# Moving the SBUF addresses of a two-block transformer kernel so that all rounded matmuls have the same distance between weights and moving columns

## What is computed

```python
# first stack, for l in range(2)
proj = rms_norm(x, attn_norm_g[l]) @ w_in[l]          # 1024 -> 8932 columns
... indexed attention (a), rwkv recurrence (b), pooling (c), retention (d)
gates = sigmoid(pg.reshape(b, s, 4, 1024) + gate_b[l])
merged = sum(gates[:, :, i] * (o_i @ w_branch[l, i]))
x = x + merged @ w_out[l]
x = x + square(relu(h2 @ mlp_up[l])) @ mlp_down[l]     # 1024 -> 4096 -> 1024

# second stack, for layer in range(2)
mod = silu(c) @ mod_w[layer] + mod_b[layer]
h = rmsnorm(x, norm_mix[layer]) * (1.0 + sc1) + sh1
y = hybrid_mixer(h, ...) if layer % 2 == 0 else mla_mixer(h, ...)
x = x + g1 * y
h = rmsnorm(x, norm_ffn[layer]) * (1.0 + sc2) + sh2
x = x + g2 * peer_ffn(h, w_q, sub_keys, u, v)

# peer_ffn: each token picks 8 x 16 of 16384 experts
act = gelu(einsum('td,ted->te', h, u[expert]))
out = einsum('te,ted->td', gates * act, v[expert])
```

## Time and profile before

| | |
|---|---|
| runs of the kernel before | 3461.89, 3463.27, 3465.05 us |
| span of the profiled execution, and its own time | 3463.0 us (nothing is shown outside the span) |
| PE busy | 3382.3 us, 98% of the span |
| PEld (weight loads, beside PE) | 3057.9 us, 88% |
| DVE, ACT, POOL busy | 71%, 47%, 10% |
| PE on the chain that ended last | 88% |
| mean granted TensorE clock | 0.989 |

### The profile page before, as it was taken

One profiled execution on the slowest core, in us unless ns is written; L12 is line 12 of the kernel. 1 busy time (PEld: TensorE's weight loads), 2 busy tenths in 40 slices (PEclk: granted clock), 3 DMA queues, 4 the chain that ended last, 5 costly groups with the idle time before them and its releaser, 6 DMA issues.

```text
span 3463.0 us, 69595 instructions
## 1 busy us (share of the span) xinstructions
PE 3382.3 (98%) x24630; PEld 3057.9 (88%) x24630; DVE 2458.7 (71%) x5105; ACT 1632.7 (47%) x3275; POOL 362.4 (10%) x480
## 2 busy tenths in 40 slices
PE   8999999999999999999999999999999999999998
PEld 7879889988888998889988888888889888888887
DVE  6734457765434866547998888888438998888887
ACT  5153355433424743145555555555445555555554
POOL 0212000020210010000460000000000540000000
PEclk9999999999999999989999999999999999999999
DMA  8633378874335985134347887888345257888875
GB/s 231 178 91 93 109 226 269 238 183 137 83 93 169 266 245 148 56 101 138 100 119 190 197 195 192 195 197 192 104 119 159 81 133 196 196 196 191 196 195 134
DMA packets 644021, 565.18 MB, mean 163 GB/s; under 512 B 62027, under 2 KB 589402, under 8 KB 643546
## 3 DMA queue, kind: packets, MB, share of 16 engines
q1 hardware_dynamic: 638564, 542.16, 59.8%
q0 software_dynamic: 4960, 19.93, 1.7%
q10 hardware_dynamic: 278, 0.08, 0.0%
HBM read 550.52 MB, written 9.44 MB: 162 GB/s over the span
## 4 chain that ended last, share of the span: by engine, by line
PE 88%; DVE 7%; ACT 2%; DMA 1%; issue 1%; SPq 1%; POOL 0%; DVEq 0%; ACTq 0%; POOLq 0%
PE bank L1473 15%; PE bank L878 15%; PE bank L856 14%; PE bank L1493 7%; PE bank L1487 7%; PE bank L1490 7%; PE bank L899 4%; PE bank L1423 3%; PE bank L1448 2%; PE bank L852 2%; DVE uT L3361 2%; PE bank L1402 1%; PE bank L1282 1%; PE bank L979 1%; PE bank L1433 1%
## 5 line engine op out<-in xcount | busy, mean ns | idle before, releaser
L1473 PE MATMUL bank<-t_high,u_parts 128*128 128x256 f32 x3072 | 425.0, 280 | 1.5 <-ACT u_parts L2212 1.5
L1473 PEld LDWEIGHTS bank<-t_high,u_parts 128*128 128x128 f32 x3072 | 403.2, 188 | 21.4 <-ACT u_parts L2212 3.6
L3400 DVE TENSOR_TENSOR v_low<-ring,v_high 128x512 fp32r<-128x512 f32 x512 | 337.0, 690 | 59.8 <-ACT v_high L2224 35.4
L1493 PE MATMUL bank<-v_low,w_high 128*128 128x512 f32 x1024 | 323.1, 397 | 0.0
L1487 PE MATMUL bank<-v_high,w_high 128*128 128x512 f32 x1024 | 318.8, 392 | 1.1 <-ACT v_high L2224 1.1
L2224 ACT ACTIVATE v_high<-ring 128x512 fp32r<-128x512 f32 x512 | 299.2, 620 | 38.4 <-PE bank L1493 38.4
L1490 PE MATMUL bank<-v_high,w_low 128*128 128x512 f32 x1024 | 316.1, 390 | 0.0
L2212 ACT ACTIVATE u_parts<-bank 128x512 fp32r<-128x512 f32 x384 | 220.0, 595 | 192.1 <-DVE bank L3372 189.0
L1776 ACT ACTIVATE arena<-bank 128x256 f32<-128x256 f32 (+1 forms) x270 | 104.1, 388 | 428.9 <-PE bank L856 235.6
L856 PE MATMUL bank<-hT,ring 128*128 128x256 f32 (+2 forms) x1232 | 279.1, 384 | 6.7 <-DVE hT L2670 6.1
L856 PE MATMUL bank<-arena,ring 128*128 128x256 f32 (+2 forms) x1168 | 272.2, 388 | 5.3 <-DVE arena L3106 3.0
(11 more groups left out here) (477 smaller groups left out, 6428.1 us busy)
## 6 DMA issues: line engine op xcount, KB each, us to landing
ring<-in_peer_v SPq DMA_DIRECT2D x256, 512.0 KB, 4.6
ring<-in_peer_u SPq DMA_DIRECT2D x768, 128.0 KB, 4.3
ring<-in_w_in SPq DMA_DIRECT2D x128, 512.0 KB, 4.0
ring<-in_mlp_up SPq DMA_DIRECT2D x64, 512.0 KB, 4.4
uT<-in_mod_w SPq DMA_DIRECT2D x64, 512.0 KB, 5.1
ring<-in_mlp_down SPq DMA_DIRECT2D x64, 512.0 KB, 4.8
ring<-in_peer_u SPq DMA_DIRECT2D x64, 512.0 KB, 3.8
arena<-in_mod_w POOLq DMA_DIRECT2D x32, 512.0 KB, 4.9
```

The costliest lines, as they stand in the source:

```text
L1473: ins = eng.matmul(PB[6 + b][:, 0:S], u_parts[:, part, k * P:k * P + P], moving[:, k, :], start=(n == 0), stop=(n == len(products) - 1))
L1493: ins = eng.matmul(PB[2 * tt + q][:, :], w_high[:, b, t], v_low[:, j % 4, d], start=False, stop=last)
L3400: tt_(v_low[:, j % 4, d], ring[:, 2 + j % 4, d], v_high[:, d].bitcast(F32), ALU.subtract).then_inc(sem("vL_ready"), 1)
```

## The change

It moves addresses and nothing else: the instructions, their order, their shapes and their waits stay. `AHEAD` is 48 floats (192 bytes), `BACK` is -80 floats (-320 bytes). The allocation order is new, with two tensors that only fill space (`before_less`, `before_selT`), and eleven overlays and areas are shifted.

```diff
+AHEAD, BACK = 48, -80
-        ring = sb("ring", [P, RING, 1024])
+        ring_all = sb("ring", [P, RING * 1024 + AHEAD])
+        ring = ring_all[:, 0:RING * 1024].rearrange("p (b n) -> p b n", n=1024)
         xT = sb("xT", [P, KD, S])
         hT = sb("hT", [P, KD, S])
         cst = sb("cst", [P, NCONST])
-        vec = sb("vec", [P, 4, P])
+        small = sb("small", [P, 128])
+        cond = sb("cond", [P, 8])
+        sb("before_less", [P, 16])
+        less_plain = sb("less_plain", [P, P])
         tab = sb("tab", [P, 2, 2, S])
-        uT = sb("uT", [P, 2, 1024])
-        selT = sb("selT", [P, 4, S])
         wT = sb("wT", [P, 2, S])
         mod = sb("mod", [P, DEPTH, MOD])
-        cond = sb("cond", [P, 8])
-        small = sb("small", [P, 128])
-        less_plain = sb("less_plain", [P, P])
+        sb("before_selT", [P, 80])
+        selT = sb("selT", [P, 4, S])
+        uT_all = sb("uT", [P, 2048 + AHEAD])
+        uT = uT_all[:, 0:2048].rearrange("p (a n) -> p a n", n=1024)
+        vec = sb("vec", [P, 4, P])
...
-        h_turned = ring[:, 6:8, :].rearrange("p b (k s) -> p (b k) s", s=S)
+        h_turned = ring_all[:, 6 * 1024 + AHEAD:8 * 1024 + AHEAD].rearrange("p (k s) -> p k s", s=S)
...
-        t_high, t_low = rounded("t_high", "hT", 0, [P, KD, S]), rounded("t_low", "ring", 6 * 1024, [P, KD, S])
+        t_high, t_low = rounded("t_high", "hT", 0, [P, KD, S]), rounded("t_low", "ring", 6 * 1024 + AHEAD, [P, KD, S])
...
-        res_s = area(12544, 4, S)
-        up_t = area(13568, 32, S)
+        res_s = area(12544 + BACK, 4, S)
+        up_t = area(13568 + BACK, 32, S)
...
-        hidden_high = rounded("hidden_high", "arena", 25856, [P, KD, S])
+        hidden_high = rounded("hidden_high", "arena", 25856 + AHEAD, [P, KD, S])
...
-        first_high, first_low = rounded("first_high", "uT", 0, [P, KD, S]), rounded("first_low", "arena", 30112, [P, KD, S])
-        second_low = rounded("second_low", "arena", 27904, [P, KD, S])
+        first_high, first_low = rounded("first_high", "uT", AHEAD, [P, KD, S]), rounded("first_low", "arena", 30080 + AHEAD, [P, KD, S])
+        second_low = rounded("second_low", "arena", 27904 + AHEAD, [P, KD, S])
...
-        g_high, g_low = rounded("g_high", "ring", 6 * 1024, [P, KD, S]), rounded("g_low", "hT", 0, [P, KD, S])
+        g_high, g_low = rounded("g_high", "ring", 6 * 1024 + AHEAD, [P, KD, S]), rounded("g_low", "hT", 0, [P, KD, S])
...
-        up_high = rounded("up_high", "arena", 0, [P, 32, S])
-        up_low = rounded("up_low", "arena", 13568, [P, 32, S])
+        up_high = rounded("up_high", "arena", AHEAD, [P, 32, S])
+        up_low = rounded("up_low", "arena", 13568 + BACK, [P, 32, S])
...
-        angle_t = area(32160, 2, S)
+        angle_t = area(32176, 2, S)
...
-        mod_sum = [arena[:, at:at + 1024] for at in (W0 + 8608, W0 + 9632, 8192, 9216, 10240, 11264)]
+        mod_sum = [arena[:, at:at + 1024] for at in (W0 + 8608, W0 + 9632, *(8192 + AHEAD + 1024 * i for i in range(4)))]
```

## The result

The changed kernel takes 3442.66 us (median of 4 runs, 3440.53 to 3443.48) against 3462.58 for the kernel before, beside which it ran: a ratio of 0.994, 95% interval 0.9926 to 0.9954. It is faster by 20 us. The forecast was 81 us. The profiled execution has a span of 3440.7 us, 22.3 us less than before.

What follows compares the result with a forecast made beforehand. TensorE (PE), busy 98% of the span, was taken as the bound, with rounded matmuls slowed by operand addresses. Terms 24.9 - 5 + 3.6 + 8.1 + 5 + 23.0 + 21.5 = 81.1 us gave 3382 us; 8-in-10 range 3312 to 3466.

Steps and rivals of the forecast that it cites:

- The addresses and what they reach: Operand distances modulo 512 bytes: before, 0, 32, 384 or 480 for rounded products; after, 320 everywhere.
- What a plain matmul costs: Chain reading: a plain float32 matmul of 256 columns takes 216 ns in two passes, so one pass costs 108 ns.
- I take half of what exceeds one pass: All rounded products: half the excess at the best offsets goes, leaving 113 ns for 256 columns, 223 for 512; chance 0.45.
- rival C: Whole kernel slower because 320 is a bad distance: 55 us more, 3518 us; chance 0.14.
- scores: Expert-loop L1473: 4608 matmuls go from 118 to 113 ns, saving 23.0 us.
- combines: Expert loop, three lines: 3072 matmuls of 512 columns go from 230 to 223 ns, saving 21.5 us.
- My last sign of being wrong: Across products: the prediction is wrong if pace gains differ between products that now all have the same distance.
- DVE's cap in the early stage: Early products: PE gains 8.8 us, but DVE, busy 87.03 of 90.00 us, lets at most 5 us through.
- DMA's cap in the MLP: MLP stages: DMA already runs at 0.88 and 0.86 of its share, so 5 us of L878's 24.9 is taken back.
- Plain matmuls unchanged: Plain matmuls whose operands move, such as L856: stay at 216 ns; at most 4.6 us loss, taken as nothing.
- (A): All rounded products: the excess is all conflict and distance 320 removes it, giving 3315 us, or 3305; chance 0.22.
- (B): Change does nothing (3463 us), or only distance-0 products gain 2 ns, 9.4 us, giving 3454; chance 0.19.

Runs made afterwards that it cites:

- The sweep: Kernel without the computation, timing only bursts of rounded matmuls at sixteen weight-to-column distances: 256 columns took 113.3 to 120.0 ns, 512 columns 226.9 to 234.2 ns.
- the second profile: The changed kernel run once more, with nothing altered, to get another profile: 3433.17 us.
- the small kernels: Kernels that leave the whole computation out and only time matmuls, at chosen distances or in alternating groups; paces were measured, no whole-kernel ratio.
- the moved pairs: Matmul-only kernel with weights and columns moved separately: all five pairs at distance 64 gave 113.3 and 117.8 ns, all three at 0 gave 120.0.

## Why the prediction was right or wrong

**What bounds the kernel: right.** PE is still 98% busy, and each ns off a matmul came out at the end except in the early stage.

**The addresses and what they reach: right.** The sweep gives at 0, 32, 384 and 480 the paces that the earlier trace rows had at the distances I derived, within about 1 ns.

**What a plain matmul costs: misread.** I took 216 ns for a whole plain matmul of 256 columns that sends its columns through twice. It is one of two records of it. The base of 108 ns for one pass, and with it the choice of 113 and 223 ns, thus rests on half a record; no run shows that one pass takes that long. The plain terms of the sum don't change by it, since no plain pace moved.

**"I take half of what exceeds one pass": this step failed, and with it the step ahead of it, that each product's own distance sets its pace.** The terms of the sum were mis-sized by it, one of them in sign. For 256 columns I took 113 ns. That pace exists, 113.3 ns, and it is the best of all distances tried. But it is one of two states at this distance, and only 0 to 98% of a product's matmuls were in it, 40% of the scores; the rest are at 117.8. For 512 columns I took 223 and got 233.0: there the sign was wrong. I had read in the earlier trace rows that the pairs at 0 were the faster ones (0.45 to 0.46 against 0.47 us) and used it for rival C only; it should have kept the combines at a loss in the sum. By term, forecast and measured: L878 19.9 and 11.3 us; first projections 3.6 and 1.6; gates 8.1 and 4.1; early 5 and 2.7; scores 23.0 and 8.8; combines 21.5 and -7.1. The combines alone are 29 of the 61 us missing, the scores 14. My last sign of being wrong came true: products that all have distance 320 gained differently, 113.4 ns in the query projection of layer 1 and 117.8 in the down projection, which was never fast in any profile. Why it never was stays open.

**DVE's cap in the early stage: right** in kind, 2.7 us of 6.7 came through, where the sum had 5. Before, L1423 had 59% of the chain in the first early stage; after, the chain there runs over DVE, in pieces like this one from 1614.77 us:

```profile
1614.77 2.30 DVE arena L3341
```

**DMA's cap in the MLP: not seen.** Where PE ran at 113.4 ns in the MLP (the second profile), it did so for 247 matmuls on end, with DMA at 0.97 of its share and 290 GB/s. The pace fell there at the transposes, not behind a wait for DMA.

**Plain matmuls unchanged: right**, 216 ns a record at distances 0 and 320.

**The rivals.** (A), all of the excess, fell: no distance gives less than 113.3 and 226.7. (B) had most of the truth for the size, and its 2 ns for products that leave distance 0 are what the down projection got (120.0 to 117.8). (C), slower, was right for 512 columns and for that width alone; its price of 7 ns for them came to 2.3. What no case had was that one product's pace depends on the product ahead of it.

The Trainium skill, page "TensorE: Matmul & The Clock Gate", section "Step-by-step: what each phase is for", has TensorE's two read ports independent, so that a weight load takes nothing from the running matmul. The sweeps speak against that: the same instructions at the same granted clock take 113.3 to 123.4 ns and 226.7 to 234.2 ns by the place of their operands alone, and in steps of 32 bytes by the difference between the two places. That it is the weight load which meets the columns is argued from this; no run streams columns without a load beside them.

## What to carry to other kernels

Measure the pace of back-to-back matmuls from start to start, per product, and compare it with a sweep of the distance between weights and moving columns for each width. Modulo 256 bytes, the best place for 256 columns (64) is a bad one for 512, whose best is 0, and moving the wide products back took 9 us more off the loops, where the whole change had taken 2. Short groups may end before their pace has settled. A pace that has two values at one address is a state; look at what stands ahead of it before you call it noise. And when a small sequence is to give the price of an insertion, take the time of the whole group from it, not the pace within.

## What the runs showed of the hardware that I had not expected

- The pace of rounded matmuls repeats with 256 bytes of distance between weights and columns: 113.3 or 117.8 ns at 64 and 320, 120.0 at 0 and 256; for 512 columns 226.9 at 0 and 256.
- At distance 64 or 320 there are two steady paces. A stop of the stream picks either (8 of 19 bursts of the moved pairs came to 117.8). Within an unbroken stream of the small kernels it is kept by wide matmuls at 64, set to 117.8 by wide ones at 0 or 192, turned over by two or more plain matmuls, and turned from 117.8 to 113.3 by small ones of some sizes (tried only behind wide ones at 0). In the big kernel eight transposes set it to 117.8, and the score groups of the changed kernel take turns, which no small sequence showed.
- A plain float32 matmul has two records in the trace, a transpose one. Each record of 256 columns takes 216 ns at distances 0 and 320, 432 for the matmul.
- 512-column matmuls at distance 0 need up to ten matmuls to settle from 236 to 227 ns behind a group that runs badly with them.
- A rounded matmul of 32 weight columns by 32 moving ones starts the next after 27 ns, but the one behind that starts 202 ns later instead of 117.
